# Splitting four late loads into a transfer of 120 partitions and one of 8 each

## The reference, cut to what matters

```python
def block(xb):                       # 128 tokens, 2 such blocks
    q = (xb @ w_q).reshape(n, PEER_HEADS, 2, PEER_HALF)          # 8 heads
    s = jnp.einsum('nhpc,hpkc->nhpk', q, sub_keys)
    ...
    best_s, best_pos = lax.top_k(cand_s, PEER_TOPK)              # 16 per head
    ids = jnp.take_along_axis(cand_i, best_pos, axis=-1)
    gate = jax.nn.softmax(best_s, axis=-1)
    u_e = u[ids]                                                 # rows of 1024
    act = jax.nn.gelu(jnp.einsum('nd,nhkd->nhk', xb, u_e), approximate=False)
    return jnp.einsum('nhk,nhkd->nd', gate * act, v[ids])
...
x = x + peer_ffn(rms_norm_2(x, g_ffn), w_peer_q, peer_sub_keys, peer_u, peer_v)
return rms_norm_2(x, g_final)
```

## Time and profile before

| what | us |
|---|---|
| time, median of 3 runs (2027.02 to 2027.5) | 2027.35 |
| span of the profiled execution, first to last instruction | 2026.2 |
| busy PE in it | 1866.7 |
| busy DVE | 1056.6 |
| busy ACT | 505.3 |
| busy POOL | 323.8 |

### The profile page before, as it was taken

One profiled execution on the slowest core, in us unless ns is written; L12 is line 12 of the kernel. 1 busy time (PEld: TensorE's weight loads), 2 busy tenths in 40 slices (PEclk: granted clock), 3 DMA queues, 4 the chain that ended last, 5 costly groups with the idle time before them and its releaser, 6 DMA issues.

```text
span 2026.2 us, 20909 instructions
## 1 busy us (share of the span) xinstructions
PE 1866.7 (92%) x8020; PEld 1381.0 (68%) x8020; DVE 1056.6 (52%) x2575; ACT 505.3 (25%) x1226; POOL 323.8 (16%) x341
## 2 busy tenths in 40 slices
PE   6999999999999999999999999998888887887777
PEld 5877788888887788888888787885343342443332
DVE  6996665401797422001201432236867677767755
ACT  2043221111214222110012545121322222222223
POOL 1000001000000000000000000013443444444441
PEclk9999999999999999999999999999999999998999
DMA  9614469844352143449552323529999999999996
GB/s 397 262 55 159 186 253 422 343 157 150 134 209 81 64 182 134 159 153 208 218 199 99 116 101 117 216 110 422 421 421 421 421 421 421 421 421 422 420 421 277
DMA packets 72435, 517.39 MB, mean 255 GB/s; under 512 B 8208, under 2 KB 8464, under 8 KB 11664
## 3 DMA queue, kind: packets, MB, share of 16 engines
q0 software_dynamic: 46384, 330.85, 40.7%
q1 hardware_dynamic: 25952, 185.21, 24.1%
HBM read 510.78 MB, written 5.24 MB: 255 GB/s over the span
## 4 chain that ended last, share of the span: by engine, by line
PE 57%; DMA 20%; DVE 18%; ACT 3%; issue 1%; POOL 1%; DVEq 0%; SPq 0%; POOLq 0%; ACTq 0%
DMA region<-in_peer_uv,small 18%; PE pj L624 12%; PE pj L887 10%; PE pj L902 9%; DVE region L1713 9%; PE st L1170 6%; PE pj L830 5%; DVE region L2125 2%; PE pj L637 2%; PE pj L931 1%; PE pj L1141 1%; DMA ring<-in_ring_w 1%; PE st L1089 1%; PE ms L830 1%; PE pj L922 1%
## 5 line engine op out<-in xcount | busy, mean ns | idle before, releaser
L1170 PE MATMUL st<-region 128*128 128x512 f32 x940 | 453.3, 631 | 111.5 <-ACT region L1549 111.5
L1170 PEld LDWEIGHTS st<-region 128*128 128x128 f32 x940 | 182.3, 200 | 361.7 <-issue 189.3
L624 PE MATMUL pj<-hT,ring 128*128 128x256 f32 x1760 | 385.0, 380 | 1.0 <-ACT region L1353 1.0
L2125 DVE CUSTOM_DVE_ANT_0 region<-region 128x1024 f32<-128x1024 f32 x235 | 287.3, 1224 | 163.7 <-DMA region<-in_peer_uv,small 161.3
L624 PEld LDWEIGHTS pj<-hT,ring 128*128 128x128 f32 x1760 | 332.6, 190 | 47.1 <-ACT region L1353 1.8
L528 POOL DMA_INDIRECT region<-in_peer_uv,small x235 | 259.4, 1104 | 393.6 <-PE st L1170 322.4
L887 PE MATMUL pj<-region,ring 128*128 128x256 f32 x1024 | 222.0, 379 | 0.5 <-DMA ring<-in_ring_w 0.5
L887 PEld LDWEIGHTS pj<-region,ring 128*128 128x128 f32 x1024 | 194.3, 190 | 28.0 <-DMA ring<-in_ring_w 0.9
L1549 ACT ACTIVATE region<-ident,small 128x128 f32<-128x128 f32 x256 | 89.2, 394 | 456.1 <-DVE small L2133 456.1
L1713 DVE SCALAR_TENSOR_TENSOR region<-region,pc 128x255 f32<-128x255 f32 (+19 forms) x528 | 202.6, 462 | 0.0
L1664 DVE TENSOR_TENSOR tmp<-xT,hT 128x256 f32<-128x256 f32 x32 | 13.6, 425 | 359.1 <-ACT hT L1249 359.1
(11 more groups left out here) (382 smaller groups left out, 1987.0 us busy)
## 6 DMA issues: line engine op xcount, KB each, us to landing
ring<-in_ring_w SPq DMA_DIRECT2D x157, 1024.0 KB, 4.8
region<-in_ada_rest POOLq DMA_DIRECT2D x40, 1024.0 KB, 12.4
region<-in_ada_first SPq DMA_DIRECT2D x8, 1024.0 KB, 18.6
region<-in_wqkv SPq DMA_DIRECT2D x2, 3072.0 KB, 12.1
region<-in_wcmp POOLq DMA_DIRECT2D x2, 2048.0 KB, 9.9
bias_dram<-region POOLq DMA_DIRECT2D x1, 4096.0 KB, 46.0
region<-in_w_o POOLq DMA_DIRECT2D x4, 1024.0 KB, 7.1
region<-in_peer_uv,small POOLq DMA_INDIRECT x235, 17.0
```

Of the source, the lines that this page charges most:

```text
L624: i = nc.tensor.matmul(b[:, m, :], w[:, k, P * m:P * m + P], hT[:, k, :], start=(k == 0), stop=(k == CT - 1))
L1170: i = nc.tensor.matmul(acc[:, u % 2, 512 * hf:512 * hf + 512], diag[:, m % NDIAG, :], uv[m % NBUF][:, D + 512 * hf:D + 512 * hf + 512], st ...
L2125: nc.vector.tensor_tensor_reduce(row, row, h_tok[:, u % 2, :], 1.0, 0.0, ALU.mult, ALU.add, dots[:, u, k:k + 1]).then_inc(sem("u_used"), 1)
```

## The change

The loads of `peer_q5`, `peer_q6`, `peer_q7` and `g_final` are each issued as two transfers, of partitions 0 to 119 and of partitions 120 to 127. Each of the two adds 16 to the semaphore, so that the counts waited for grow by 16 for these loads. Nothing else is changed.

```diff
--- before.py
+++ after.py
@@ -61,6 +61,7 @@
 QUERY_AT = {h: 2 * TOPK * (h - AHEAD) + 8 if h >= AHEAD else 2 for h in range(1, PH)}
 SCORES_AT = {h: QUERY_AT[h] + (10 if h >= AHEAD else 7) for h in range(1, PH)}
 RETRIEVED = {u: [TOPK * (u - AHEAD) + k for k in (3, 7, 11)] for u in range(3, 2 * PH)} | {1: [4, 5, 6], 2: [13, 15, 17]}
+LATE = [(f"peer_q{j}", 2, 0) for j in range(PH - 3, PH)]
 WIDE = 48
 G_MIX2, G_MEM2, POOL_SC2 = 0, 8, 16
 UNITS = [(g, s) for g in range(G) for s in range(2)] + [("x", 0), ("x", 1)]
@@ -356,7 +357,7 @@
         full_at = []
         for n, j in enumerate(jobs):
             before = full_at[n - RING] if n >= RING else 0
-            full_at.append(before + 16)
+            full_at.append(before + (32 if j in LATE else 16))
 
 
         MERGE_BANKS, GATE_BANK, banks = [], None, 60 * DEPTH + 2
@@ -385,6 +386,12 @@
         @block.sync
         def _(sp):
             sp.dma_start(c_act, a["c"].partition_broadcast(P)).then_inc(sem("c_in"), 16)
+
+            def load_split(dst, src, done):
+
+                for lo, hi in ((0, 120), (120, P)):
+                    sp.dma_start(dst[lo:hi], src[lo:hi]).then_inc(done, 16)
+
             n = 0
             for what in EARLY:
                 if what == "x":
@@ -417,13 +424,16 @@
             for n, (name, l, j) in enumerate(jobs):
                 if n >= RING:
                     sp.wait_ge(sem("slot_used"), n - RING + 1)
-                    sp.dma_start(ring[:, n % RING, :], a["ring_w"][n]).then_inc(ring_full[n % RING], 16)
+                    if (name, l, j) in LATE:
+                        load_split(ring[:, n % RING, :], a["ring_w"][n], ring_full[n % RING])
+                    else:
+                        sp.dma_start(ring[:, n % RING, :], a["ring_w"][n]).then_inc(ring_full[n % RING], 16)
                 if name == "w_in" and j == 3:
                     load_layer(l)
 
 
             sp.wait_ge(sem("slot_used"), len(jobs))
-            sp.dma_start(g_fin, a["g_final_2"].partition_broadcast(P)).then_inc(sem("g_fin_in"), 16)
+            load_split(g_fin, a["g_final_2"].partition_broadcast(P), sem("g_fin_in"))
             sp.wait_ge(sem("u_used"), SLOTS)
             for n, (s, lo, hi) in enumerate(((0, 0, D), (1, 0, 512), (1, 512, D))):
                 sp.wait_ge(sem("out_ready"), n + 1)
@@ -2133,7 +2143,7 @@
                     nc.vector.scalar_tensor_tensor(wgt[:, u, k:k + size], wgt[:, u, k:k + size], gsum[:, u:u + 1], gate[:, u, k:k + size],
                                                    ALU.mult, ALU.mult).then_inc(sem("wgt_ready"), 1)
                 if n == SLOTS - TOPK + 11:
-                    dve.wait_ge(sem("g_fin_in"), 16)
+                    dve.wait_ge(sem("g_fin_in"), 32)
                     final_norm(0)
             final_norm(1)
```

## The result

The changed kernel takes 2043.71 us (median of 4 runs, 2043.29 to 2044.15) against 2027.42 us for the kernel before in the same session: ratio 1.0078, 95% interval 1.0065 to 1.0092. It is 16.3 us slower, where 2028.4 us had been forecast, within what a measurement can tell from no change, and the time lies above the range, whose upper end was 2032.0 us.

The account below looks back on a forecast made before the run. The gather stage was taken as DMA-bound, its end set by one late engine. 2027.35 us plus 1.09 us for that engine's ninth rows, with issues and row order at 0, gave 2028.4 us; range 2020.3 to 2032.0 us.

Parts of the forecast that it names:

- The order within a load: Four split loads: engines get other partitions than for gather rows; priced at 0, upper end 8.8 us, each load's time doubled.
- the crowding rival: Gather stage: engines writing the same partitions slow loads and gathers, 4.4 us more, 2032.9 us in all; chance 0.17.
- all costs seen, 2.50 and 1.28 us, are those of the bytes alone: Gather stage before the change: 2.50 us per ring load and 1.28 us for the scale, for the engine that ends last.
- What bounds the kernel: Gather stage: DMA engines always busy at 421 GB/s, 2.48 us per gather; the engine ending last sets the end.
- Which engine is late: End of gather stage: the engine working alone about 7 us carries one row of any 8-partition transfer.
- the mark of the gate biases: Second layer: groups of three small packets mark engines carrying a bias row; the engine delayed by DVE's fetch showed one.
- The spared engine's rival: Four loads: the 120 rows skip the engine that ends last, gaining up to about 7 us, 2020.8 us; chance 0.28.
- Why that engine is late: Gather stage: DVE's own instruction fetches each put about 1 us on that engine, which has no idle time to recover.
- The late engine's share, 9 rows for 8: Four loads: the engine that ends last carries a ninth row, +0.31 us on three loads, +0.16 on the scale, +1.09 us.
- one engine alone for 8 us rather than 7: Tail of the gather stage: sign that the forecast is right, with the other engines' end staying near 2007.6 us.
- The issues at 0: SP's queue: 8 transfers issued for 4, 0.33 us each, 1.3 us in all, costed at 0 because loads come long before use.

## Why the prediction was wrong

**The step that failed is "The order within a load".** It asked the right question and answered it with 0, and its upper end was mis-sized: it doubled only the load's own rows for the late engine, 8.8 us for all four, and the crowding rival took half of that, 4.4 us. The runs show 15.8 us. A load of 1 MB slows everything that the sixteen engines write while it lasts, the gathers too: packets of 0.53 us for 0.31 in the middle of it, and 3.2 MB moved in the 12 us of the stretch, for which 421 GB/s need 7.6 us. Each costs 4.4 to 4.8 us, the scale 2.0. Doubling had to be applied to the load and to as many gather rows that go out between its rows: 2 x 8.8 = 17.6 us, near the 15.8. The reason given for 0, that "all costs seen, 2.50 and 1.28 us, are those of the bytes alone", came from transfers of 128 rows only: the rows I called nearest were of the one kind in which no crowding shows.

What bounds the kernel was right. The gather stage is DMA-bound at a beat of 2.48 us, the late engine has no idle time, and so a loss there comes out at the end one for one: 15.7 us of missing rate and 15.8 to 16.3 us of time.

Which engine is late was right. It carries a row of a transfer of 8, as the mark of the gate biases said, and extra rows on the eight move the end: 4.2 us by the ratio 1.0021, for 4.8 us of work. The spared engine's rival was therefore wrong for the reason given. Why that engine is late was not tried: no run removed one of DVE's fetches. The trace before fits the prediction's account in that the lateness gathers bit by bit: counted by the completions (the packets under 512 B) at DVE's starts, the other engines lead by roughly 2 us on average at 1493 us and by roughly 8 us at 1988 us.

The Trainium skill ("DMA: Bandwidth & Descriptors", "Latency and other measured facts") names engines 7 and 15 as usually slower. By the Trainium skill's same page, which gives a transfer of SP the lowest-numbered engines, copies of 7 rows go to 0 to 6. In these runs copies of 7 rows slow the end as those of 8 do (2032.84 and 2032.48 us), so by that numbering the late engine is neither 7 nor 15.

The late engine's share, 9 rows for 8, is by these runs right too, but its 1.09 us cannot be seen beside the crowding; no run here isolates it. The sign that was to show it, one engine alone for 8 us rather than 7, was not a good one: seven other engines carry a ninth row as well, and the late one is then no further behind them. It was alone for 7 us. The issues at 0 were right: the cut by columns issues as many and costs nothing that can be told (its interval is 2 us either way).

The rival "the loads get in the gathers' way" was the case that came. It had been given a chance of 0.17. Its mechanism was right as far as the runs show it, and its size too small by more than a factor of three. The Trainium skill, "SBUF — State Buffer", section "Door 1: The DMA port swizzle", gives 16 ports of 8 partitions each, four neighbours and the four 32 further on, with the other half of the partitions on other ports. If each of the fifteen engines takes a run of 8 neighbours, which the trace does not show, that rule puts their first four rows on eight of the ports, and the next four on the other eight. The runs agree in the order and the direction: nothing for whole columns, 9.5 us for runs of 7, 15.8 us for runs of 8 with the row of eight, 27.6 us for sixteen neighbours at a time. The traces show rates and not ports: that the crowding is on the SBUF side is shown, that it is these ports is argued from the Trainium skill's page.

Not tried: a cut that spares one engine and leaves each of the others its own partitions.

## What to carry to other kernels

When a stage is bound by DMA, load whole tiles of 128 partitions, and if a load must be cut, cut it by columns: that cost nothing that could be told (ratio 0.9989 to 1.0008), while cuts by partitions cost 2.7 to 7.9 us for each MB here (9.5 and 27.6 us over 3.5 MB). A DMA share of 1 says that the engines are occupied, not that they move data; read the GB/s beside it. And where an operation is new to the trace, price it together with everything that shares its resource while it runs, not by the nearest row of a kind that does not show the problem.

## What the hardware showed that I had not expected

A copy between two stretches of HBM whose rows join end to end is dealt out to 16 engines whatever its rows: 8 rows of 8 KB went out as 16 packets, and 120 rows as 16. With 256 bytes left out of each row it went to as many engines as 8, 7 and 15.

Eight rows of 8 KB written by eight engines into eight neighbouring partitions, 0.23 MB over the four loads, cost some 4 to 5.5 us (the missing rate and the ratios) in a stage where the same bytes take 0.55 us at 421 GB/s.
